# Identity products in front of four waits of TensorE at the start of a transformer block

## The reference, cut to what matters

```python
c_act = jax.nn.silu(c)
mod = c_act @ ada_w[l] + ada_b[l]
sh1, sc1, g1, sh2, sc2, g2 = jnp.split(mod, 6, axis=-1)
h = modulate(rms_norm(x, norm1_w[l]), sh1, sc1)      # h * (1 + scale) + shift
z = h @ w_in[l]
```

## Time and profile before

| | us |
|---|---|
| median of 3 runs | 1915.15 |
| lowest and highest | 1910.86, 1916.44 |
| span of the profiled execution, first to last instruction | 1911.6 |
| time of the profiled execution itself | not recorded apart from its span |

### The profile page before, as it was taken

How to read it: one execution, slowest core, us unless ns; L and a number is a source line. 1 busy time by engine, 2 the same in 40 slices (tenths; PEclk the granted TensorE clock), 3 DMA queues, 4 the chain that set the end, 5 groups by cost and what they waited for, 6 DMA issues and landing times. The chain is left out here.

```text
span 1911.6 us, 24238 instructions
## 1 busy us (share of the span) xinstructions
PE 1840.5 (96%) x8636; PEld 1524.3 (80%) x8636; DVE 1116.5 (58%) x1665; ACT 679.9 (36%) x1218; POOL 986.7 (52%) x607
## 2 busy tenths in 40 slices
PE   3989999999999999999999998989999999999998
PEld 3778788888888878888888887867888888878887
DVE  5834756454554666766565548584556455656636
ACT  5643241323233323223332232454444444432123
POOL 1786634344351777775536342339788878800000
PEclk8999999999999999999999999999999999999999
DMA  9066732111020544434222126613454444399764
GB/s 332 33 176 193 227 110 47 45 29 50 24 66 14 204 150 154 165 115 154 71 77 71 44 74 252 214 34 88 154 161 136 156 152 162 115 392 367 292 226 171
DMA packets 186531, 272.18 MB, mean 142 GB/s; under 512 B 10281, under 2 KB 122825, under 8 KB 186193
## 3 DMA queue, kind: packets, MB, share of 16 engines
q1 hardware_dynamic: 176466, 243.20, 38.6%
q10 hardware_dynamic: 9984, 27.91, 4.0%
HBM read 194.23 MB, written 76.85 MB: 142 GB/s over the span
## 5 line engine op out<-in xcount | busy, mean ns | idle before, releaser
L1218 PE MATMUL ps<-b_hT,b_w_split 128*128 128x512 f32 x2528 | 627.9, 396 | 3.2 <-POOL b_w_split L1001 1.7
L1218 PEld LDWEIGHTS ps<-b_hT,b_w_split 128*128 128x128 f32 x2528 | 461.6, 189 | 92.5 <-issue 2.1
L998 POOL TENSOR_TENSOR b_spare<-b_w_stage 1x1 f32<-1x1 f32 x66 | 20.1, 304 | 406.2 <-PE ps L1218 315.7
L1176 POOL TENSOR_TENSOR b_wu<-b_raw,b_wu 128x512 fp32r<-128x512 f32 x110 | 166.9, 1526 | 55.4 <-ACT b_wu L2264 54.8
L999 POOL TENSOR_SCALAR b_w_split<-b_w_stage 128x1024 fp32r<-128x1024 f32 x66 | 182.8, 2770 | 0.0
L2501 DVE TENSOR_TENSOR b_macc<-ps,b_macc 128x512 f32<-128x512 f32 x188 | 122.6, 686 | 75.2 <-PE ps L1299 45.0
L1001 POOL TENSOR_TENSOR b_w_split<-b_w_stage,b_w_split 128x1024 fp32r<-128x1024 f32 x66 | 161.4, 2445 | 5.5
L2501 DVE TENSOR_TENSOR b_cb<-ps,b_snap 128x512 f32<-128x512 f32 x66 | 45.4, 687 | 166.0 <-PE ps L1741 165.3
L2171 ACT ACTIVATE b_probs<-b_probs,b_smax 128x128 f32<-128x128 f32 (+3 forms) x64 | 49.8, 778 | 193.3 <-DVE b_smax L2903 193.3
L1739 PE MATMUL ps<-b_db,b_da 128*128 128x512 f32 x280 | 109.8, 392 | 2.6 <-DMA b_da<-f_units 2.6
L1740 PE MATMUL ps<-b_db,b_da 128*128 128x512 f32 x280 | 109.5, 391 | 0.0
(11 more groups left out here) (319 smaller groups left out, 3986.6 us busy)
## 6 DMA issues: line engine op xcount, KB each, us to landing
f_units<-b_fu SPq DMA_DIRECT2D x70, 512.0 KB, 2.6
b_w_stage<-in_w_in SPq DMA_DIRECT2D x53, 512.0 KB, 4.1
down_units_d<-b_wd SPq DMA_DIRECT2D x66, 256.0 KB, 2.0
b_da<-f_units SPq DMA_DIRECT2D x11, 1536.0 KB, 6.4
b_macc<-in_ada_w SPq DMA_DIRECT2D x32, 512.0 KB, 4.8
b_dr<-down_units_d SPq DMA_DIRECT2D x14, 1024.0 KB, 9.9
b_da<-f_units SPq DMA_DIRECT2D x7, 2048.0 KB, 7.9
b_wd<-in_w_down SPq DMA_DIRECT2D x11, 1024.0 KB, 5.1
```

Source lines behind the costliest of these rows:

```text
L998: pool.tensor_tensor(spare[0:1, :], src[0:1, 0:1], src[0:1, 0:1], ALU.add)
L1176: pool.tensor_tensor(wu[:, n % RING, 1, :], src, f(wu[:, n % RING, 0, :]), ALU.subtract).then_inc(u_rdy, 1)
L1218: return pe.matmul(o, l, r, start=start, stop=stop)
```

## The change

Four runs of products of `identR` by `identR`, 160 in all, are put into PE's program. All write the first 128 columns of bank 3, and nothing reads them. 88 stand ahead of `vectors(0)`, 44 ahead of `vectors(1)`, 14 ahead of unit 5 and 14 ahead of unit 6 of the transposes. No wait and no signal is added, and no other engine's program is changed.

```diff
+            def kept_warm(n):
+
+                for _ in range(n):
+                    mm(ps[:, 3, 0:P], identR[:, :], identR[:, :], True, True)
+
+            kept_warm(88)
             vectors(0, 0, range(KT))
             norm_transposes(0, range(4))
+            kept_warm(44)
             vectors(1, 2, range(2))
             vectors(1, 1, range(2, KT))
-            norm_transposes(0, range(4, KT))
+            norm_transposes(0, (4,))
+            kept_warm(14)
+            norm_transposes(0, (5,))
+            kept_warm(14)
+            norm_transposes(0, (6, 7))
```

## The result

| | before | changed |
|---|---|---|
| median of 13 runs each, us | 1913.91 | 1919.25 |
| lowest and highest | 1908.99, 1916.44 | 1915.73, 1928.64 |
| changed over before | | 1.0037, 95% interval 1.0024 to 1.0051 |
| span of the profiled execution | 1911.6 | 1926.8 |

A forecast was written before the change was run, and what follows sets the result against it. TensorE, busy 96% of the span, was taken as the bound. 0 (88) + 0 (44) + 0 (14 + 14) - 0.55 = -0.55 us; on the median, 1915.15 - 0.55 = 1914.6 us, range 1909.8 to 1919.2.

The forecast's parts named there:

- The 88: Ahead of `vectors(0)`: 12 to 32 slow, ending at 21.2 to 23.4 us, middle 22.3; hidden, cost 0.
- rival 3: All four runs: identity products never raise the clock, `first_jobs` at 59.7, 16 us later, 1931 us; chance 0.06.
- The costs of 0 for the 44 and the 14s: Ahead of `vectors(1)` and units 5 and 6: at full clock 5.0 us and 1.6 us each, hidden in TensorE's waits.
- 67 of them slow: Among the 88 ahead of `vectors(0)`: the number slow at which they end behind 24.9 us and begin to cost.
- the range: Whole kernel: 1909.8 to 1919.2 us, said to take in the full 2.2 gain, rival 4 and three runs' spread.
- rival 4: Opening: fetching 320 more instructions comes late, the 88 end near 30.8 us, DVE's copy 4.6 late, 1919.7; chance 0.05.
- the row at 89.67: Behind the opening: read as TensorE waiting for POOL, whose start moved by the same 0.55 us.
- The prices: Each 128x128 product on TensorE: 0.113 us at full clock, between 0.215 and 0.245 at the low one, 0.225 taken.
- The reading of the clock: Opening: TensorE at 1.2 GHz from its first product to about 29 us, though the view prints 1.00 ahead of 32.5.
- The point at which it decides: Ahead of `vectors(0)`: cover is gone when it ends behind 28.4 us, needing the 88 to end behind 24.9.
- Rival 2: At the first transposes: the clock falls again, some 22 of the 44 slow, cost 0.2 to 0.7, 1915.6 us; chance 0.15.
- What is gained: Units 6 and 7 and large products: 2.2 us, of which 1.6 become a wait for ACT; about 0.55 left.

The follow-up runs named there:

- the repeat: The changed kernel run once more with no edit: one run, 1922.64 us.
- the kernel with twelve products at the start: 12 products of 128x512 rows of x put ahead of `vectors(0)` in the 512-column kernel that had none there: 1911.89 us, ratio 0.9993.
- rows of `x`: The changed kernel with its 88, 44, 14 and 14 products of 128x128 taken from rows of x instead of the identity: 1920.01 us, ratio 1.0034.
- the kernel without the first run: The kernel with 36, 20, 6 and 6 products of 128x512 rows of x, without the 36 ahead of `vectors(0)`: 1910.59 us, ratio 0.9980.
- the wide kernel: The changed kernel with 36, 20, 6 and 6 products of 128x512 rows of x instead of its 160 identity products: 1916.13 us, ratio 0.9996.
- the kernel with fewer products: The changed kernel with 52 and 14 identity products ahead of the two vectors and none ahead of units 5 and 6: 1913.77 us, ratio 0.9997.
- the 44 alone: The kernel before with only the 44 identity products ahead of `vectors(1)`: 1914.11 us, ratio 1.0006.

## Why the prediction was wrong

**The step that failed** is in the prediction's part "The 88": "How many are slow can't be read. The large products were given the clock 2.7 us after they began; the opening's own small work, 21.70 to 28.9, went 7.2 us without it [...] With those as ends: 12 slow and 76 fast [...] 32 slow and 56 fast". All 88 were slow, in every one of the four profiles with 88 products of this size. I took the two rows as ends of one scale of time, when they were two forms of work. The large products were 128x512; the work that went 7.2 us without the clock had 1 or 128 columns behind each load of 128 weights, and the 88 are of that kind. The row nearest in form was the second, and it gave only a least time, no upper end. The cost of 0 for the 88 came from this bracket, and so did the 0.06 for rival 3. The costs of 0 for the 44 and the 14s rested on the same clock: in the profiled execution they took 9.63 and 3.23 us each, where I had 5.0 and 1.6.

**Two sums** were wrong besides. "67 of them slow" took the others as free: with them at 0.113, the 88 end behind 24.9 us from about 46 slow ones on, nearer to the 32 of my bracket than I wrote. And the range, said to take in rival 4 and the spread of three runs, ended at 1919.2, under rival 4's own 1919.7 and with no spread in it. A third point is a reading: the row at 89.67 has [0.21 <-issue], so it doesn't show TensorE waiting for POOL there.

**The prices** held: 0.214 us a slow product (I took 0.225; the lower bound was 0.215), and (40.21 - 35.10)/44 = 0.116 us for the 44 of the repeat, the first one or two of them slow (I took 0.113). **The reading of the clock** ahead of 32.5 us, 1.2 GHz against a printed 1.00, held: in the kernel with twelve products at the start the clock has records from its fall at 17.2 on, it is 0.50 over `vectors(0)`, and these take 3.57 us there against 3.54 before.

**The point at which it decides** was not contradicted, though nothing was run close to it: the first run should hurt from an end behind 24.9 us; 52 identity products ended at 21.1 and 88 of 256 columns at 22.7, and neither cost anything in the times, while 88 that ended at 28.7 made DVE 3.8 us late.

**Rival 3** is what happened, in the profiled execution almost by its own numbers (`first_jobs` at 57.23, said 59.7). Its price of 16 us was too high as the typical one: in the repeat the clock rose among the 44, the opening lost 6.9 us, and the median of 13 runs is 5.3 us above before. **Rival 2** had the clock up before the first transposes and lost in them, and that didn't happen. A loss of the clock later on, with TensorE at work, did: at 42.3 in the repeat and at 43.6 with rows of `x`.

**What is gained** held where the clock was raised without making `x` late. Said: `first_jobs` at 42.65, units 8 and 9 at 51.1 behind a new wait of about 1.5 us for ACT. Measured in the kernel without the first run: 42.68, 51.08, 1.33 us. That is 0.6 us. The ratio of 0.9980 is 3.8 us, which the opening doesn't explain. Its profile is 3.4 us shorter than that of before, and one execution each can't say how much of the other 2.8 is a habit of the kernel.

**The transposes.** In the wide kernel the clock rose at 28.28, when TensorE had done nothing but transposes since 25.46. It rose during or close behind the same 16 in the repeat, with rows of `x` and in the kernel with fewer products too, but not behind those of the profiled execution or of the 44 alone, and what tells these apart is open. The Trainium skill (TensorE: Matmul & The Clock Gate, Part 4: PE-mode transpose) says that transposes don't count as products do. The trace of the wide kernel doesn't agree with it.

**Code that comes late** (rival 4) didn't happen: there is no gap among the 160.

## What to carry to other kernels

Filler work in front of a wait is safe only if it ends in time at the slow clock: count it at the price that it has when it fails to do what it is for. Take the form of the filler from the rows that did raise the clock, here 256 or 512 columns for each load of weights; 128 did not do it in 19 us. And look first at what is waited for behind the slow stretch: in the best kernel, units 8 and 9 could have started 1.9 us earlier than before, and 1.3 of these went straight into a wait for ACT.

## What the runs showed of the hardware that I had not expected

- Dense 128x128 fp32r products, identity or rows of `x` alike, ran 19.0 us at the low clock with no gap between them (415 ns each, one every 0.214 us) in four profiles. 128x256 products in the same count and place ran 12.6 us in all.
- The clock could fall with TensorE at work: it fell at 42.3 us in the repeat of the change and was 0.50 from 45 to 50, and at 43.6 us with rows of `x`, with no gap on TensorE ahead of it or behind.
- It could rise while TensorE did nothing but transposes: at 28.28 us in the wide kernel, 2.8 us after the first of them.
- Products of 128 columns of weights and 1 column ran at 1.95 us for 16 records at full clock against 3.51 to 3.58 at the low one. Their 16 loads of weights did the same: 1.98 us in all in the kernel with no products ahead of `vectors(0)`, against 3.49 in the kernel before.
- A run of early products that lasted to 20.6 us or longer came with `x` about 1.2 us late at ACT (36.6 to 37.3 against 35.5 to 35.8), though the transfer was asked for only at about 26 us.
